# Pages of a paged cache fetched by SyncE, one transfer per page, in place of row gathers by GpSimd

## What is computed

```python
def one(args):
    qs, kvs, pages, buf = args
    past = pool[layer, pages].reshape(past_len, 4, N_KV, HEAD_DIM).astype(jnp.float32)
    ...
    return nsa_sequence(qs, past_len, rows, win, w_c1, w_c2, pe, slopes)
...
k_cmp = compress_rows(rows[:, 0], pe[0], w_c1[0], w_c2[0])
v_cmp = compress_rows(rows[:, 1], pe[1], w_c1[1], w_c2[1])
...
_, idx = lax.top_k(imp, n_top)
k_sel = k_blk[kv_idx, idx].reshape(qb, N_KV, n_top * SLC_BLOCK, HEAD_DIM)
```

## Time and profile before

| | |
|---|---|
| median of three runs | 2531.56 us |
| profiled execution, its time / its span | 2521.44 / 2519.7 us |
| PE busy | 2134.0 us, 85% |
| DVE, ACT, POOL busy | 1361.3, 916.0, 650.8 us |
| mean granted TensorE clock | 0.847 of full speed |
| stretch of the samples' compression | about 1001 to 1309 us |
| stretch of the samples' attention | about 1366 to 1550 us |

### The profile page before, as it was taken

One profiled execution on the slowest core, in us unless ns is written; L12 is line 12 of the kernel. 1 busy time (PEld: TensorE's weight loads), 2 busy tenths in 40 slices (PEclk: granted clock), 3 DMA queues, 4 the chain that ended last, 5 costly groups with the idle time before them and its releaser, 6 DMA issues.

```text
span 2519.7 us, 28151 instructions
## 1 busy us (share of the span) xinstructions
PE 2134.0 (85%) x10468; PEld 1634.1 (65%) x10468; DVE 1361.3 (54%) x1765; ACT 916.0 (36%) x1229; POOL 650.8 (26%) x467
## 2 busy tenths in 40 slices
PE   5997677899999766888884567889999999999995
PEld 3754334799964454544442334778888888888884
DVE  4404674277720333555543112456777777787775
ACT  0112001000000112554541322156677666677663
POOL 1000000000020012333325552024545443345522
PEclk8995556799999556998985777789999999999997
DMA  7422021345671012333325554458899998899983
GB/s 267 140 84 56 6 50 55 117 134 164 179 256 64 9 31 61 109 109 94 108 75 182 179 170 131 143 202 301 316 326 324 328 328 315 315 343 348 325 323 138
DMA packets 227688, 453.70 MB, mean 180 GB/s; under 512 B 11831, under 2 KB 175839, under 8 KB 226306
## 3 DMA queue, kind: packets, MB, share of 16 engines
q1 hardware_dynamic: 199274, 347.55, 39.3%
q0 software_dynamic: 28320, 104.90, 13.7%
HBM read 439.60 MB, written 21.27 MB: 183 GB/s over the span
## 4 chain that ended last, share of the span: by engine, by line
PE 70%; DVE 8%; issue 5%; ACT 3%; another core or an unknown queue 2%; DMA 1%; DVEq 0%; POOLq 0%; POOL 0%; ACTq 0%; SPq 0%
PE bank L2105 62%; PE bank L2108 8%; ACT arena L2601 2%; DVE arena L1311 1%; ACT L2601 1%; DVE uT L2364 0%; DMA arena<-in_w_moe_gu 0%; DVE arena L2499 0%; DMA ring<-scr_y,mkv 0%; DVE arena L796 0%; DVE rtmp L2357 0%; ACT ring L2601 0%; ACT arena_r L2601 0%; DVE arena L809 0%
## 5 line engine op out<-in xcount | busy, mean ns | idle before, releaser
L2105 PE MATMUL bank<-arena_r 128*128 128x448 f32 (+4 forms) x3656 | 928.2, 358 | 18.5 <-DVE uT_r L650 11.3
L2105 PEld LDWEIGHTS bank<-arena_r 128*128 128x128 f32 (+1 forms) x3656 | 680.3, 196 | 98.1 <-DVE uT_r L650 11.8
L2105 PE MATMUL bank<-arena 128*128 128x512 f32 (+19 forms) x1594 | 409.0, 465 | 120.9 <-DVE arena L1311 36.9
L1609 DVE TENSOR_TENSOR ring_r<-ring,arena_r 128x1792 fp32r<-128x1792 f32 (+2 forms) x168 | 400.8, 2413 | 94.9 <-ACT arena_r L2601 94.9
L2601 ACT ACTIVATE arena_r<-ring 128x1792 fp32r<-128x1792 f32 (+1 forms) x216 | 369.5, 1725 | 186.4 <-PE bank L2105 181.2
L2601 ACT ACTIVATE arena<-bank 64x256 f32<-64x256 f32 (+11 forms) x512 | 210.7, 415 | 563.3 <-PE bank L2105 253.2
L2105 PEld LDWEIGHTS bank<-arena 128*128 128x128 f32 (+12 forms) x1594 | 221.8, 214 | 238.0 <-issue 140.4
L1971 POOL TENSOR_TENSOR ring_r<-ring,arena_r 128x1792 fp32r<-128x1792 f32 (+1 forms) x48 | 212.5, 4427 | 460.9 <-ACT arena_r L2601 460.9
L2105 PE MATMUL bank<-ring_r,arena_r 128*128 128x448 f32 (+1 forms) x840 | 292.2, 373 | 0.0
L2108 PE MATMUL bank<-consts_sb,arena 128*128 128x128 f32 (+9 forms) x780 | 152.2, 329 | 122.3 <-ACT arena L2601 26.8
L1931 POOL DMA_INDIRECT ring<-in_cache_nsa,arena x176 | 167.0, 949 | 281.6 <-PE bank L2108 230.9
(11 more groups left out here) (343 smaller groups left out, 2035.3 us busy)
## 6 DMA issues: line engine op xcount, KB each, us to landing
ring<-in_w_moe_gu SPq DMA_DIRECT2D x144, 896.0 KB, 6.9
ring<-in_w_moe_d SPq DMA_DIRECT2D x60, 1024.0 KB, 6.4
arena<-in_w_moe_gu SPq DMA_DIRECT2D x48, 896.0 KB, 6.0
ring<-in_w_ffn_gu SPq DMA_DIRECT2D x22, 1024.0 KB, 7.1
ring<-in_w_in_a SPq DMA_DIRECT2D x8, 1536.0 KB, 7.7
arena<-in_w_moe_d SPq DMA_DIRECT2D x12, 1024.0 KB, 6.4
ring<-in_w_ffn_d SPq DMA_DIRECT2D x8, 1408.0 KB, 7.1
out_win_s<-in_cache_nsa_win POOLq DMA_DIRECT2D x1, 8176.0 KB, 43.7
```

The lines of the kernel that those rows point to most:

```text
L1609: V.tensor_tensor(unit_low(c), unit_slot(c), unit_high(c), ALU.subtract).then_inc(S("m_sp"), 1)
L2105: return nc.tensor.matmul(out, lhsT, rhs, start=first, stop=last, **kw_)
```

## The change

GpSimd's 256 gathers go. SyncE gets a function `page_loads`, which stands in its queue after the early weight loads, and reads each sample's 16 page numbers from SBUF into registers. For a half of the compression it issues 16 transfers, one per page: 8 partitions, 8 rows of 2 KB in each. For `past(b)` with b % 3 not 0 it issues 16 transfers of 8 partitions with 16 rows of 2 KB each, for b % 3 = 0 twice as many, of 8 rows each. The prompt's two loads into `gat` move to SyncE as well. The page table is loaded once, into one partition, instead of 8 times, and VectorE's step that made row numbers (`idx`) goes. The waits ahead of each fetch are the same as before, on the other engine, except that `past(2)` now stands behind the four `sel4` loads in the queue. The windows stay with GpSimd.

```diff
-            for s in range(8):
-                load("ld_pt", pages[s:P:8, :], I["page_table"].rearrange("b n -> n b"), allow_slow_non_contiguous=True)
+            load("ld_pt", pages, I["page_table"].rearrange("(o b) n -> o (b n)", o=1))
...
-            def gather(dst, b, l, kinds, name):
-                pool.indirect_dma_start(dst, None, rows, bass.IndirectOffsetOnAxis(ap=idxb[:, b:b + 1], axis=0),
-                                        element_offset=(2 * l + kinds) * 512).then_inc(S(name), 16)
...
+            def page_numbers(b):
+                _, numbers = nc.values_load_multi_w_load_instructions(
+                    pages[0:1, NPAGES * b:NPAGES * b + NPAGES], engines=(mybir.EngineType.SP,), min_val=0, max_val=NPOOL - 1,
+                    skip_runtime_bounds_check_because="the reference indexes its pool with the same table")
+                return numbers
+            def page(number, kinds, l0, l1):
+                rows = I["cache_nsa"][0, number].rearrange("(s l) k g d -> s l (k g d)", l=CST)
+                return rows[:, l0:l1, 512 * kinds:512 * kinds + 512]
+            def past(b):
+                for j, number in enumerate(page_numbers(b)):
+                    parts = slice(8 * j, 8 * j + 8)
+                    if b % 3:
+                        sp.dma_start(gsl[parts, b % 3 - 1, :, :], page(number, 1, 0, CST)).then_inc(S(f"ld_g{b % 3}"), 16)
+                    else:
+                        for half in range(2):
+                            sp.dma_start(gat[parts, half, :, :], page(number, 1, 8 * half, 8 * half + 8)).then_inc(S("ld_g0"), 16)
+            sp.wait_ge(S("st_rows"), 32)
+            sp.wait_ge(*done("bg_mm", 3))
+            segs = O["rows_p"][0, 0].rearrange("(s l) k g d -> s l (k g d)", l=CST)
+            for half in range(2):
+                sp.dma_start(gat[0:TP // CST, half, :, :], segs[:, 8 * half:8 * half + 8, 0:512]).then_inc(S(f"ld_c{half}"), 16)
+            sp.wait_ge(S("ld_pt"), 16)
+            for c in range(1, TS + 1):
+                numbers = page_numbers(c - 1)
+                for half in range(2):
+                    sp.wait_ge(S("ct"), 16 * (c - 1) + 8 * half + 8)
+                    for j, number in enumerate(numbers):
+                        sp.dma_start(gat[8 * j:8 * j + 8, half, :, :], page(number, 0, 8 * half, 8 * half + 8)).then_inc(S(f"ld_c{half}"), 16)
+            sp.wait_ge(S("ct"), 16 * (TS + 1))
+            past(0)
+            sp.wait_ge(S("vv2"), TS + 1)
+            sp.wait_ge(S("p_oe"), 2 * NQ)
+            past(1)
...
+            past = page_loads(sp)
             sp.wait_ge(*done("imp"))
             sp.dma_start(scr_imp, imp.rearrange("p b j -> p (b j)")).then_inc(S("st_imp"), 16)
...
+            past(2)
+            for b in range(2, TS - 1):
+                sp.wait_ge(S("pv_mm"), b - 1)
+                past(b + 1)
             sp.wait_ge(S("pv_mm"), TS - 1)
```

More of the change, by code:

```diff
@@ L56 @@
         "pre0", "mt_s", "bd0", "qk_done", "n_s", "bd", "hsq", "ms_q0", "ms_d0", "ms_p0", "ms_pte0", "mixm0", "u_split0",
-        "bg_ev", "idx", "ms_q1", "ms_d1", "ms_p1", "ms_pte1", "mixm1", "qr_ev", "pc_d0", "pc_w", "pc_oe", "q12", "pc_d",
+        "bg_ev", "ms_q1", "ms_d1", "ms_p1", "ms_pte1", "mixm1", "qr_ev", "pc_d0", "pc_w", "pc_oe", "q12", "pc_d",
         "pc_p", "pc_s", "imp", "pct_ev", "sel", "oc_ev", "pz0", "cm_d", "cm_f", "cm_g", "mixT", "ur_0", "rank", "rt_d", "y_at",
@@ L472, in build @@
         g12 = area(NQ, 3, TS)
-        pages = area(P, TS).bitcast(I32)
-        idxb = area(P, TS).bitcast(I32)
+        pages = area(1, TS * NPAGES).bitcast(I32)
         q12 = area(HD, TS, NKV, NQ)
@@ L1005, in turn @@
                 if n % 10 == 0:
-                    pe.wait_ge(S(f"ld_g{b % 3}"), 256 * (b // 3 + 1))
+                    pe.wait_ge(S(f"ld_g{b % 3}"), 16 * NPAGES * (2 if b % 3 == 0 else 1) * (b // 3 + 1))
                 if n % 10 == 8:
@@ L1227, in turn @@
                 if n % 8 == 0:
-                    pe.wait_ge(S(f"ld_c{half}"), 16 if c == 0 else 16 + 128 * c)
+                    pe.wait_ge(S(f"ld_c{half}"), 16 + 16 * NPAGES * c)
                 if N >= 2:
@@ L1415, in layer_b_dve @@
             link(V.tensor_copy(hconst, bank[4][0:HD, 0:2]), "kn_ev")
-            dve.wait_ge(S("ld_pt"), 128)
-            link(V.tensor_scalar(idxb, pages, 256.0, C("seg"), ALU.mult, ALU.add), "idx")
             mem_attend_dve(dve, link, V, 1)
@@ L1916, in layer_b_pool @@
             store(O["win_s"][0, :, WBUF - 1].rearrange("b k g d -> b (k g d)"), kvS[:, 4:6, :].rearrange("p k d -> p (k d)"), "st_win")
[L1917 to L1921, removed]
             pool.wait_ge(S("st_mem"), 128)
@@ L1925, in layer_b_pool @@
             load("ld_d12", d12b, I["dist12"])
-            rows = I["cache_nsa"][0].rearrange("a r (u k) g d -> (a r u) (k g d)", u=2)
-            def gather(dst, b, l, kinds, name):
-                pool.indirect_dma_start(dst, None, rows, bass.IndirectOffsetOnAxis(ap=idxb[:, b:b + 1], axis=0),
-                                        element_offset=(2 * l + kinds) * 512).then_inc(S(name), 16)
[L1934 to L1943, removed]
             def window(b):
                 load(f"ld_win{b % 2}", winb[b % 2], I["cache_nsa_win"][0, b].rearrange("(p r) k g d -> p r (k g d)", r=4))
[L1947 to L1951, removed]
             pool.wait_ge(*done("oc_ev"))
@@ L1955, in layer_b_pool @@
             window(1)
-            pool.wait_ge(S("st_sel"), 16)
-            past(2)
             for b in range(2, TS):
@@ L1960, in layer_b_pool @@
                 window(b)
-                if b + 1 < TS:
-                    past(b + 1)
             pool.wait_ge(*done("wob_ev", KT))
@@ L1993, in layer_b_pool, with page_loads @@
                                             bass.IndirectOffsetOnAxis(ap=yidx[0:rows, r, i:i + 1], axis=0)).then_inc(S(f"ld_y{i}"), 16)
+        def page_loads(sp):
+            def page_numbers(b):
[31 more added lines that the diff above has]
+            past(1)
+            return past
         def moe_load(sp):
```

## The result

| | before | after |
|---|---|---|
| median of the runs | 2531.28 us | 2719.86 us (2718.42 to 2727.62) |
| ratio, with its 95% interval | | 1.0756 (1.0723 to 1.0789) |
| span of the profiled execution | 2519.7 us | 2725.8 us |
| `past(0)` starts (compression done) | 1308.7 us | 1359.0 us |
| `imp` sets out for HBM | 1355.1 us | 1465.0 us |

The account below looks back on a forecast made before the run. It took PE's work to bound the kernel, gathers hidden, and transfers into few partitions to bind afterwards: compression +6, attention +97, PE's holds 0 to -28, total +104 (rounded with the parts) on the median 2531.6, 2636 us; range 2465 to 2920.

Parts of the forecast that it names:

- likeliest case: Page fetch: two pages overlap at 119 GB/s, giving 2636 us; own range 2561 to 2726 us, chance 0.42.
- The bound is the transfer into few partitions, not the issue: SyncE's page fetch: 0.44 us a transfer and 4.4 us for 16 numbers don't bind; the transfer rate decides.
- Two pages at a time, 119 GB/s: Page transfers: two pages of 8 rows overlap, so a half takes 17.6 us and a `past` 35.2 us.
- the first rival: Page transfers: one page at a time at 60 GB/s, compression +207, attention +380, time 3119 us; chance 0.13.
- the rule cited with it: The Trainium skill's port rule: four neighbouring partitions share one port of 27.2 GB/s, making 54 GB/s for one page.
- Compression +6: Compression: a half takes 19.6 us with landing against intervals of 20.6; only the short intervals are passed, +6 us.
- The trip of `imp` waits for the data of both pasts: SyncE's queue in the attention: `imp` starts 30 us later if it waits for both pasts' data; counted so.
- PE's holds, at most 60 us: PE's stops without source during gathers: 28.2 us in compression, 32.2 us in attention; compression's counted 0 to -28.
- The fast rival: Page fetch: eight engines full at 207 GB/s, fetch hidden and PE's stops gone, 2476 us; chance 0.22.
- The stretch that the change touches: Span from about 940 to 1550 us, where the page cache is fetched; the other four fifths stay as they are.
- Clock and relief of POOL at 0: PE's possibly halved clock in a slower attention and POOL's saved gather work: each counted as 0 us.
- the case between, 80 GB/s throughout (2847): Page transfers at 80 GB/s: compression +80, attention +235, 2847 us; chance 0.15 for rates between 95 and 60 GB/s.

Follow-up runs that it names:

- e4_stride4: The changed kernel with each page's 8 rows in partitions 4 apart instead of neighbouring: 2473.4 us, ratio 0.9802 to the kernel before.
- e5_stride16: The changed kernel with each page's 8 rows in partitions 16 apart instead of neighbouring: 2632.72 us, ratio 1.0408 to the kernel before.
- e2_compression_only: The changed kernel with the past gathered by GpSimd again, only the compression's halves fetched by SyncE: 2570.19 us, ratio 1.0135 to the kernel before.
- e8_trip_by_pool: The changed kernel with the `imp` and `sel` transfers moved from SyncE's to GpSimd's queue: 2643.0 us, ratio 1.0515 to the kernel before.
- e9_plain_loads: The kernel before with each of GpSimd's 256 gathers replaced by an ordinary load of the same size from fixed pages: 2376.13 us, ratio 0.9473.
- e3_order: The changed kernel with pages issued in the order 0, 4, 1, 5, 2, 6 and so on: 2881.69 us, ratio 1.1406 to the kernel before.
- e10_mixed: The kernel before with each 128-row gather split into an ordinary load of 112 rows and a gather of 16: 2476.47 us, ratio 0.9798.

## Why the prediction was right in its direction and short in its size

It said 2636 us, slower, with 2561 to 2726 for its likeliest case; 2719.86 lies inside, near the end. That it lies inside is in part luck: few stretches flowed at the 119 GB/s of that case, and slow stretches (58 to 70) and fast ones (152 to 186) made up for one another. Step by step:

- *The bound is the transfer into few partitions, not the issue.* Right. While the queue had room, transfers of 64 rows started 0.46 us apart (1302.69 to 1307.31, ten steps) where 0.44 was counted; 128 rows took at least 0.67 us each, more than counted and still below what the data took. The 16 numbers cost 1.5 to 1.8 us ahead of a `past`, not 4.4. `e4_stride4` and `e5_stride16` show that the partitions set the rate.
- *Two pages at a time, 119 GB/s.* This is the term that was mis-sized, and not by one factor. At the start of a stream nothing overlaps: the first two pasts took 134.5 us for 8.39 MB (62 GB/s) where the sum had 4.4 + 70.4 + 2 = 76.8, 58 us of the shortfall. I had argued that nothing makes pages wait for one another, but the rate says that there they don't overlap. The rate of the first rival, 60 GB/s, was right for this stretch, and the rule cited with it; for the rest of the attention it was wrong. The last six pasts, from 1507.9 to 1745.7, took 237.8 us where the sum had 211 + 12.6 + 2 = 225.6.
- *Compression +6.* Measured +50.3. After each gap the stream starts anew at 68 to 70 GB/s (1130 and 1285), stays at 69 for 50 us more (1140 to 1190), then brings 90 (1205 to 1260), and comes to 118 to 145 only shortly before a gap (1265 and 1115). The half's 17.6 us were counted at 119; at 69 it takes 30 and at 90 it takes 23, above the interval of 20.6. `e2_compression_only` shows these 50 us as 43 on the median. And the holds, which I had left at 0 to -28, did go (no part of the chain is without source); that PE then wants the halves earlier, and waits the more for rows, is my reading.
- *The trip of `imp` waits for the data of both pasts.* The branch that I took was right (28.5 us to land). It came at 1465.0 where the sum had about 1386, because of the two terms above. Moving the trip out of the queue is worth 61 us (`e8_trip_by_pool`), where the prediction's own branch was worth 30; the stream is faster then, for a reason that stays open.
- *PE's holds, at most 60 us.* Wrong, though this time it hardly shows, since PE waits for rows instead. I had read only the part without source in the earlier trace rows and passed over the "issue" beside it, 17.0% and 14.5%, as PE's own. I had also taken the sample period of 26.7 us as PE's, into which the gathers just fit; it was made by the gathers. `e9_plain_loads` puts the whole at some 130 us. And the window from 1328 to 1348, which I had cited for the holds, says little: in `e9_plain_loads`, without gathers, PE is about as idle at that stage (3.41 of 10 us, 1269 to 1279). The fast rival's 2476 is near the 2473.4 of `e4_stride4` by luck: that is a compression 42 us shorter and an attention that lasts as before, bound by SyncE's issue and the eight engines. With all 16 engines it is 2381.62.
- *The stretch that the change touches.* 935 to 1550 us are a quarter of the span, not a fifth, and of the right-hand 15 slices three stand at 8 and 5 tenths; nothing hangs on either.
- *Clock and relief of POOL at 0.* PE's busy time is 2116 us against 2134, so a clock that is lower on average (0.824 against 0.847) cost nothing that shows.
- *Of the rivals*, one page at a time (3119) holds for the first two pasts and for parts of the compression; the case between, 80 GB/s throughout (2847), was too slow for the later ones.

Together: 50.3 - 6 = 44 us in the compression, 58 in the first pasts, 12 in the later ones, less 4 for a trip of 14.3 instead of 18.8 from the landing of the pasts to the start of the third (the numbers took less): 110 us more than forecast up to the last row (213 against 103). On the median it is 84: 7 us don't reach the span, and 18 us are how the two profiled executions stand to their medians (10 under it before, 8 above it after).

## What to carry to other kernels

Before one cuts a load into a transfer per page, one asks how many partitions each piece reaches and how far apart they are: 8 neighbours brought some 60 GB/s at a stream's start, the same 8 rows 4 partitions apart 150 and later up to 205, a page over all partitions 387. Rows that are spread cost the issuing engine more (0.69 us a transfer instead of 0.28), and that can become the next bound. A queue that is full of slow transfers also delays every small one behind it, so a latency trip belongs on another queue. And when a profile shows "issue" or an unknown source on a busy engine only while another engine's transfers run, its share is to be counted as the price of those transfers, by replacing them once with plain ones.

## What the runs showed that I had not expected

- The rate of a stream of 8-row transfers isn't fixed: with the same 8 engines occupied (share 0.53) it was about 60 to 70 GB/s behind each gap and up to 182 late in the attention. Running on isn't enough for it: it stayed at 64 for 130 us in the first two pasts (1360 to 1490). The order of pages changes how far it comes (`e3_order`, 101 GB/s in mid-attention). What lifts it is open.
- The issue of a 64-row transfer by SyncE took 0.28 us into 8 neighbouring partitions, 0.60 us 16 apart and 0.69 us 4 apart.
- While GpSimd's gathers by index run, PE's own instructions come more slowly (8 matmuls in 6 us instead of 0.61), besides its stops. Fetching by them cost this kernel some 130 us, in a place where it looked hidden; in the compression the cost goes with their rows (`e10_mixed`). What inside the chip does it is open.
